# A streaming-encoder block on one core: the first weights behind two token tiles, the first products in three passes, and half of one remainder on GpSimd

## The chip, the cores and the metric

The kernel runs on one core of a Trainium2 chip. The time is that of one launch in device microseconds, the median of several runs. The engines run side by side, each through a list of its own, and meet only at semaphores: TensorE (PE in the profile, its weight loads PEld), VectorE (DVE), ScalarE (ACT), GpSimd (POOL) and SyncE (SP), which issues the DMAs.

## The reference

512 tokens of 1024 features pass one layer. All tensors are float32.

```
u = RMSNorm(h)                                    # 512 x 1024
q, k, v, z, xBC, dt, gate_a, gate_b = split(u @ w_in)
A = banded attention with sinks(rope(q), rope(k), v) @ w_attn_out
B = (SSD scan over silu(conv(xBC)), dt; y * silu(z), group RMSNorm) @ w_ssd_out
h = h + RMSNorm(merge(A, B) @ w_out)
f = silu(conv(gate)) * conv(value), of RMSNorm(h) @ w_up
h = h + RMSNorm(f @ w_down)
```

## The kernel before

**Products in three parts.** Each float32 operand is split into a rounded part and the remainder. Of the weights these are `whi` (rounded by ScalarE, a copy of `raw`, L452) and `wlo` (VectorE subtracts, `raw` minus `whi`, L797), of the normed tokens `uhi` and `ulo`. Every product is three matmuls: rounded by rounded, remainder by rounded, rounded by remainder (L1204 to L1206 where the tokens are the stationary operand, L1197 to L1199 where the weights are).

**Weight blocks.** The weights come in blocks of at most 128x2048, numbered through the whole kernel, into two slots in turn. Per block: SyncE loads it, ScalarE rounds it (`hi`), VectorE takes the remainder (`lo`), TensorE multiplies. Semaphores count them: `hi_done`, `lo_done`, `blk_done`. SyncE waits for `lo_done` before it loads into a slot again, ScalarE for `blk_done` before it overwrites one.

**The groups.** The mixer runs in four groups (`G`), each of seven blocks: 0 and 1 are q, k, v (in group 0 also dt), 2 to 4 the convolved columns, 5 and 6 the gate z, where block 5 holds the first half of the contraction and block 6 the second. After block 4 a group goes through four token tiles of 128 (`t`). In tile 0 TensorE does, in this order: transposes `tok(0)` and `tok(1)`, sums of decays, the products of z with block 5, the attention scores, transposes `tok(2)` to `tok(4)` (L1319), the products of z with block 6, and the products `y` (L1416), which need `decay_m` after its mask (L968) and `xdt` (L974). `tok(4)` needs `silu(5)` and the masked `cb_m` from VectorE.

**The work beside it in tile 0.** VectorE finishes the convolutions (`taps`, L899), multiplies `silu` (L908: `tanh_c` by `conv`), builds `cb_m` (L959), masks `decay_m` twice, takes the remainder of block 6 (`lo_next(5)`), and then does softmax and `xdt`. ScalarE: `tanh`, `tok` copies, exponentials, the rounding of block 6 (`hi_next(5)`). GpSimd: the products `seg_lo` (`build`, L386), two for each tile, then `xdtd` and `xd` (L406, L408).

**The beginning.** SyncE issues two tiles of x, small parameters, two more tiles of x, and then block 0 (four DMAs). Per token tile: ScalarE squares, GpSimd takes the inverse root (`root_x`), VectorE scales (`scale_x`, L823), TensorE transposes (L1214), VectorE applies the norm's weight (`weigh_x`, L812), ScalarE rounds (`u_hi`, L463), and VectorE (first four feature blocks, `rest_x`, L819) and GpSimd (last four, L374) take the remainder. GpSimd also works out the angles for rope (L358 to L369) on which ScalarE's sines wait (L488, semaphore `ang_ok`). After these ScalarE does `hi_next(1)`, the rounding of block 2.

Of the kernel before, what the change touches and what calls it, by code (L numbers as in the profile page):

```python
# [21 lines left out]
def hybrid_block(nc, x, positions, mix_pre_norm, w_in, attn_sinks, ssd_conv_w, ssd_conv_b, ssd_dt_bias,  # L22
# [47 lines left out]
    with ctx:  # L70
# [86 lines left out]
        for name in (  # L157
            "x_in0", "x_in1", "x_in2", "x_in3", "consts_in", "par_in", "par2_in", "posT_ok", "pool_c", "loaded0", "loaded1", "hi_done", "lo_done", "blk_done",
            "band_zero", "dve_chain", "pool_chain", "xsq", "rstd", "xn", "xT_mm", "u_plain", "uhi_ok", "u_ok", "u2_ok", "parT_mm", "par_ok",
            "ang_ok", "rope_tab", "hp_ok",  # L160
            "qkv_mm", "qkv_sb", "roped", "va_ok", "dtabs", "dtexp", "dt_ok", "decay_mm", "decay_ok",
            "qkT_mm", "qkT_sb", "conv_mm", "tapped", "conv_ok", "tanhed", "silu_ok", "tok_mm", "tok_sb",
            "seg_hi_ok", "seg_lo_ok", "seg_mm", "lexp", "cb_mm", "cbm_ok", "s_mm", "smx", "sexp", "p_ok", "z_mm", "ztanh", "zg_ok",
            "m_ok", "pT_mm", "pT_sb", "y_mm", "y_done", "xdt_ok", "xdtd_ok", "xd_ok", "st_mm", "st_ok", "w_ok", "wsq",
            "yrstd", "yn_ok", "yT_mm", "yT_sb", "o_mm", "o_sb",
            "split_hi", "split_lo", "ga_mm", "ga_tanh", "at_mm", "at_ok", "gb_mm", "gb_tanh", "so_mm", "so_ok",
            "mg_hi", "mg_lo", "mg_lo2", "res_in", "out_mm", "d_sq", "d_rstd", "d_h", "h_sq", "h_rstd", "hn_ok", "hT_mm", "h_plain", "h_hi", "h_ok",
            "up_mm", "ftap", "fconv", "ftanh", "f_ok", "fhi_ok", "flo_ok", "fpar_ok", "dn_mm", "e_sq", "e_rstd", "e_ok", "stored",
        ):
# [139 lines left out]
        def _(pool):  # L309
# [44 lines left out]
            w0, w1 = tanh_c[:, 0, :], tanh_c[:, 1, :]
            NA = NT * HALF
            r3 = lambda a: a.rearrange("p (t k) -> p t k", t=NT)
            pool.wait_ge(s["posT_ok"], 1)
            link(pool.tensor_tensor(r3(w0[:, 0:NA]), small[:, 12:16].unsqueeze(2).to_broadcast([P, NT, HALF]),  # L358
                                    inv[:, :].unsqueeze(1).to_broadcast([P, NT, HALF]), ALU.mult))
            link(pool.tensor_scalar(w1[:, 0:NA], w0[:, 0:NA], 1.0 / 6.283185307179586, MAGIC, ALU.mult, ALU.add))  # L360
            link(pool.tensor_scalar(w1[:, 0:NA], w1[:, 0:NA], -MAGIC, None, ALU.add))
            for c in TWO_PI:
                link(pool.tensor_scalar(w1[:, NA:2 * NA], w1[:, 0:NA], -c, None, ALU.mult))
                link(pool.tensor_tensor(w0[:, 0:NA], w0[:, 0:NA], w1[:, NA:2 * NA], ALU.add))
            link(pool.tensor_scalar(w0[:, 0:NA], w0[:, 0:NA], PI, -PI, ALU.min, ALU.max))
            link(pool.tensor_scalar(w1[:, 0:NA], w0[:, 0:NA], 0.0, None, ALU.min))
            link(pool.tensor_scalar(w1[:, NA:2 * NA], w0[:, 0:NA], 0.0, None, ALU.max))
            link(pool.tensor_tensor(w1[:, NA:2 * NA], w1[:, NA:2 * NA], w1[:, 0:NA], ALU.subtract))
            pool.tensor_scalar(w0[:, NA:2 * NA], w1[:, NA:2 * NA], -1.0, 1.5707963267948966, ALU.mult, ALU.add).then_inc(s["ang_ok"], 1)  # L369

            for t in range(NT):
                pool.wait_ge(s["uhi_ok"], t + 1)
                c = slice(t * P, (t + 1) * P)
                pool.tensor_tensor(ulo[:, KD // 2:, c], plain(t)[:, KD // 2:, :], uhi[:, KD // 2:, c].bitcast(F32),  # L374
                                   ALU.subtract).then_inc(s["u2_ok"], 1)
# [408 lines left out]
        def _(dve):  # L784
# [101 lines left out]
            def group(i, p):  # L886
# [300 lines left out]
        def _(pe):  # L1187
# [41 lines left out]

            pe.wait_ge(s["par2_in"], 16 * 10)  # L1230
            pe.wait_ge(s["u_plain"], 2)
            pe.transpose(ps[:, 3, 0:NR1], prow[0:NR1, 1, :], ident[0:NR1, 0:NR1]).then_inc(s["parT_mm"], 1)
            pe.transpose(ps[:, 3, NR1:NR1 + P], prow[:, 2, :], ident[:, :]).then_inc(s["parT_mm"], 1)
            pe.transpose(ps[:, 3, NR1 + P:NR1 + P + NCP], prow[0:NCP, 0, :], ident[0:NCP, 0:NCP]).then_inc(s["parT_mm"], 1)

# [6 lines left out]
            def group(i, p):  # L1242
# [381 lines left out]
```

## Time and profile before

| | |
|---|---|
| median of 3 runs | 1083.49 us (1082.47 to 1083.94) |
| the profiled execution: its own time | 1083.09 us |
| its span, first to last instruction | 1081.4 us |
| TensorE busy | 1051.6 us, 97% |
| VectorE, ScalarE, GpSimd busy | 649.9, 454.6, 130.7 us |
| mean granted TensorE clock | 0.996 |

Read it so: the profiled execution lies 0.4 us under the median of the runs, and its span 1.7 us under its own time. TensorE is idle for under 30 us in all, so what another engine does counts only where TensorE waits for it.

### The profile page before, as it was taken

Reading aid. Unit: us, or ns where it says so; the run is one execution under the profiler, and the core shown is the slowest. Engines: PE = TensorE matmul, PEld = TensorE weight load, DVE = VectorE, ACT = ScalarE, POOL = GpSimd, SP = SyncE. Lnnn points to the kernel's source line nnn. Section 1 sums busy time; section 2 is a strip of 40 time slices with the busy share of each in tenths; the row PEclk is TensorE's granted clock in tenths of the full one; section 3 lists DMA queues with packets and bytes.
Section 4 is the critical chain, followed back from the end, with each engine's and each line's share of the span. In section 5 each row is a group of like instructions: output and inputs, shape, how many; then the busy total and the mean of one; then the engine's idle time right before and its main releaser. Section 6 shows DMA issues by size and latency. Waiting matters only on the chain.

```text
span 1081.4 us, 13741 instructions
## 1 busy us (share of the span) xinstructions
PE 1051.6 (97%) x5295; PEld 883.5 (82%) x5295; DVE 649.9 (60%) x863; ACT 454.6 (42%) x714; POOL 130.7 (12%) x200
## 2 busy tenths in 40 slices
PE   6999999999999999999999999999999999999997
PEld 5987887888779877888888888788888888888886
DVE  6788777876776777842433233466666666651214
ACT  6465456536654565532321213363434444431112
POOL 7113300330043013200000003120000000000001
PEclk8999999999999999999999999999999999999999
DMA  6321132114202420233233343412423333333221
GB/s 190 116 68 30 40 118 68 30 40 122 82 12 62 134 78 2 78 98 97 78 117 97 97 162 130 136 40 78 113 81 110 84 107 87 104 96 111 82 75 78
DMA packets 108426, 95.39 MB, mean 88 GB/s; under 512 B 12175, under 2 KB 98523, under 8 KB 108379
## 3 DMA queue, kind: packets, MB, share of 16 engines
q1 hardware_dynamic: 108379, 94.74, 28.8%
q8 instruction: 32, 0.52, 0.2%
q14 instruction: 15, 0.12, 0.0%
HBM read 92.63 MB, written 2.10 MB: 88 GB/s over the span
## 4 chain that ended last, share of the span: by engine, by line
PE 91%; DVE 5%; ACT 2%; DMA 1%; issue 1%; POOL 0%; DVEq 0%; POOLq 0%; SPq 0%; ACTq 0%
PE ps L1197 18%; PE ps L1199 18%; PE ps L1198 18%; PE ps L1204 9%; PE ps L1206 9%; PE ps L1205 9%; PE ps L1416 3%; DVE wlo L797 1%; PE ps L1412 1%; PE ps L1364 1%; PE ps L1428 1%; PE ps L1437 1%; DVE conv L899 1%; DVE conv L908 1%; PE ps L1239 1%
## 5 line engine op out<-in xcount | busy, mean ns | idle before, releaser
L797 DVE TENSOR_TENSOR wlo<-raw,whi 128x2048 fp32r<-128x2048 f32 (+2 forms) x83 | 188.7, 2275 | 213.2 <-ACT whi L452 213.2
L1197 PE MATMUL ps<-uhi,whi 128*128 128x512 f32 x640 | 249.6, 390 | 0.0
L1199 PE MATMUL ps<-uhi,wlo 128*128 128x512 f32 x640 | 249.1, 389 | 0.0
L1198 PE MATMUL ps<-ulo,whi 128*128 128x512 f32 x640 | 249.0, 389 | 0.0
L452 ACT ACTIVATE whi<-raw 128x2048 fp32r<-128x2048 f32 (+2 forms) x83 | 155.2, 1871 | 173.4 <-PE ps L1206 93.0
L1199 PEld LDWEIGHTS ps<-uhi,wlo 128*128 128x128 f32 x640 | 120.1, 188 | 25.0
L1197 PEld LDWEIGHTS ps<-uhi,whi 128*128 128x128 f32 x640 | 120.1, 188 | 24.8 <-DVE wlo L797 0.2
L1198 PEld LDWEIGHTS ps<-ulo,whi 128*128 128x128 f32 x640 | 120.1, 188 | 24.7
L1204 PE MATMUL ps<-whi,uhi 128*128 128x512 f32 (+2 forms) x320 | 122.2, 382 | 9.9 <-DVE wlo L797 9.9
L1206 PE MATMUL ps<-wlo,uhi 128*128 128x512 f32 (+2 forms) x320 | 119.3, 373 | 0.0
L1205 PE MATMUL ps<-whi,ulo 128*128 128x512 f32 (+2 forms) x320 | 119.2, 373 | 0.0
L1145 DVE SCALAR_TENSOR_TENSOR yT<-ps,fpar,yT 128x511 f32<-128x511 f32 x88 | 65.7, 749 | 37.6 <-ACT yT L754 36.0
L1204 PEld LDWEIGHTS ps<-whi,uhi 128*128 128x128 f32 x320 | 60.9, 190 | 18.2 <-ACT x_tok L521 8.8
L754 ACT ACTIVATE yT<-ps,fpar 128x512 f32<-128x512 f32 x44 | 34.2, 780 | 98.9 <-DVE fpar L1140 68.0
L1197 PE MATMUL ps<-rhi,whi 128*128 128x512 f32 x192 | 74.8, 390 | 0.0
L1199 PE MATMUL ps<-rhi,wlo 128*128 128x512 f32 x192 | 74.7, 389 | 0.0
L1198 PE MATMUL ps<-rlo,whi 128*128 128x512 f32 x192 | 74.7, 389 | 0.0
L1204 PE MATMUL ps<-whi,rhi 128*128 128x512 f32 x176 | 68.5, 389 | 0.0
L1205 PE MATMUL ps<-whi,rlo 128*128 128x512 f32 x176 | 68.5, 389 | 0.0
L1206 PE MATMUL ps<-wlo,rhi 128*128 128x512 f32 x176 | 68.5, 389 | 0.0
L1206 PEld LDWEIGHTS ps<-wlo,uhi 128*128 128x128 f32 x320 | 60.9, 190 | 7.9
L1205 PEld LDWEIGHTS ps<-whi,ulo 128*128 128x128 f32 x320 | 61.0, 191 | 7.0
(220 smaller groups left out, 1437.7 us busy)
## 6 DMA issues: line engine op xcount, KB each, us to landing
raw<-in_w_in_dram SPq DMA_DIRECT2D x24, 1024.0 KB
raw<-in_w_up_dram SPq DMA_DIRECT2D x44, 512.0 KB
raw<-in_w_down_dram SPq DMA_DIRECT2D x11, 1024.0 KB
raw<-in_w_in_dram SPq DMA_DIRECT2D x16, 512.0 KB
raw<-in_w_ssd_out_dram SPq DMA_DIRECT2D x8, 1024.0 KB
raw<-in_w_attn_out_dram SPq DMA_DIRECT2D x4, 1024.0 KB
raw<-in_w_out_dram SPq DMA_DIRECT2D x4, 1024.0 KB
yT<-in_x_dram SPq DMA_DIRECT2D x4, 512.0 KB, 5.2
```

What stands on the lines that cost most here:

```text
L452: act.activation(whi[sl][:, 0:width] if into is None else into, raw[sl][:, 0:width], ACT.Copy).then_inc(s["hi_done"], 1)
L754: act.activation(work[:, v, :], bank(2 * q + v), ACT.Identity, scale=fpar[:, q, FTAPS - 1, v:v + 1], bias=fpar[:, q, FTAPS, v:v + 1]).then ...
L797: dve.tensor_tensor(wlo[sl][:, 0:width] if into is None else into, raw[sl][:, 0:width], h.bitcast(F32), ALU.subtract).then_inc(s["lo_done" ...
L899: ins = dve.scalar_tensor_tensor(out=conv[:, f, sh:], in0=ps[:, 4 + f % 4, 0:S - sh], scalar=cw[:, k, at:at + 1], in1=conv[:, f, sh:], op0 ...
L1145: ins = dve.scalar_tensor_tensor(out=work[:, v, sh:], in0=ps[:, 2 * q + v, 0:S - sh], scalar=fpar[:, q, k, v:v + 1], in1=work[:, v, sh:], ...
L1197: pe.matmul(bank(b)[:, span], hi_[:, k, c], ah[:, span], start=first and k == 0, stop=False)
L1198: pe.matmul(bank(b)[:, span], hi_[:, k, c], al[:, span], start=False, stop=False)
L1199: ins = pe.matmul(bank(b)[:, span], lo_[:, k, c], ah[:, span], start=False, stop=last and k == KD - 1)
L1204: pe.matmul(o, ah, wh, start=first, stop=False)
L1205: pe.matmul(o, al, wh, start=False, stop=False)
L1206: return pe.matmul(o, ah, wl, start=False, stop=last)
L1416: ins = pe.matmul(ps[:, 5 if t else 6, c_], decay_m[:, h, :], xdt[:, c_], start=True, stop=True)
```

## The change

**In the groups.** ScalarE rounds block 6 right after `tok(0)` (`hi_next(5)`), ahead of `tanh(5)`, `tok(1)` and the exponentials. VectorE takes the remainder of the first half of that block alone (1024 of 2048 columns), between `silu(4)` and `silu(5)`; GpSimd takes that of the other half, between `build(0)` and `build(1)`, and counts in `zlo2_ok`. TensorE waits for `zlo2_ok` before the products with block 6, and SyncE before it loads into that slot.

**At the beginning.** Block 0 is issued ahead of token tiles 2 and 3. Its remainder is split between VectorE and GpSimd (832 columns each). TensorE's products with block 0 go tile by tile in three passes of four matmuls, with the transposes of tiles 2 and 3 and of the parameters between them. ScalarE rounds block 0 ahead of its squares of tiles 2 and 3. GpSimd works `root_x`, its part of the token remainders (L356 after the change), the half block and the angles in a new order, with the large memset first.

```diff
@@ SyncE, put(n)
+                if n == 2:
+                    sp.wait_ge(s["wlo0_ok"], 1)
+                if n <= N_C1 + 1 and n % PER_G == 1 and n > 1:
+                    sp.wait_ge(s["zlo2_ok"], n // PER_G)
@@ SyncE, beginning
-            for t in range(2, NT):
-                sp.dma_start(xin[:, t, :], x2[t * P:(t + 1) * P, :]).then_inc(x_in[t], 16)
...
                     if g == 0 and h == 0:
+                        for t in range(2, NT):
+                            sp.dma_start(xin[:, t, :], x2[t * P:(t + 1) * P, :]).then_inc(x_in[t], 16)
                         late_parameters()
@@ GpSimd, beginning
+            root_x(0)
+            root_x(1)
+            pool.wait_ge(s["posT_ok"], 1)
...
+            pool.wait_ge(s["hi_done"], 1)
+            half = slice(2 * QKV0, 4 * QKV0)
+            pool.tensor_tensor(wlo[0][:, half], raw[0][:, half], whi[0][:, half].bitcast(F32), ALU.subtract).then_inc(s["wlo0_ok"], 1)
+            root_x(2)
+            rest_x(0)
+            root_x(3)
+            rest_x(1)
+            for n, c in enumerate(TWO_PI):
+                link(pool.tensor_scalar(w1[:, NA:2 * NA], w1[:, 0:NA], -c, None, ALU.mult))
+                link(pool.tensor_tensor(w0[:, 0:NA], w0[:, 0:NA], w1[:, NA:2 * NA], ALU.add))
+                if n:
+                    rest_x(n + 1)
@@ GpSimd, group
                 build(0)
+                sl = (G * PER_G + 6) % 2
+                pool.wait_ge(s["hi_done"], G * PER_G + 7)
+                pool.tensor_tensor(wlo[sl][:, BLK // 2:], raw[sl][:, BLK // 2:], whi[sl][:, BLK // 2:].bitcast(F32),
+                                   ALU.subtract).then_inc(s["zlo2_ok"], 1)
@@ ScalarE, beginning
+            hi(0, 64, None, 4 * QKV0)
             square_x(2)
+            u_hi(0)
             square_x(3)
-            u_hi(0)
-            hi(0, 64, None, 4 * QKV0)
             u_hi(1)
+            u_hi(2)
@@ ScalarE, group
                 tok(0)
+                hi_next(5)
+                tanh(5)
                 act.wait_ge(s["xd_ok"], G * NT)
                 tok(1)
-                tanh(5)
...
                     if t == 0:
-                        hi_next(5)
@@ VectorE, beginning
             weigh_x(0)
+            weigh_x(1)
             scale_x(2)
+            rest_x(0)
+            lo(0, 1, 2 * QKV0)
             scale_x(3)
-            weigh_x(1)
-            rest_x(0)
-            lo(0, 1, 4 * QKV0)
+            rest_x(1)
             weigh_x(2)
-            rest_x(1)
             weigh_x(3)
@@ VectorE, group
                 silu(4)
+                lo_next(5, BLK // 2)
                 silu(5)
...
                         mask_decays(range(2))
-                        lo_next(5)
@@ TensorE, beginning, first_block()
+                pe.wait_ge(s["hi_done"], 1)
+                rounded_rounded(0)
+                rest_rounded(0)
+                rounded_rounded(1)
+                turn_x(2)
+                pe.wait_ge(s["lo_done"], 1)
+                pe.wait_ge(s["wlo0_ok"], 1)
+                rounded_rest(0)
+                rest_rounded(1)
+                rounded_rest(1)
+                turn_x(3)
+                turn_parameters()
+                rounded_rounded(2)
+                rest_rounded(2)
+                rounded_rest(2)
...
+                rounded_rounded(3)
+                rest_rounded(3)
+                rounded_rest(3).then_inc(s["blk_done"], 1)
@@ TensorE, group
                             sl = block_ready(5 + h)
+                            if h:
+                                pe.wait_ge(s["zlo2_ok"], G + 1)
```

How VectorE's list stands in group 0 around tile 0, before (L797 is the remainder of block 6, L908 silu, L959 `cb_m`, L968 the masks, L985 the start of softmax):

```order
L899 SCALAR_TENSOR_TENSOR conv<-ps,par,conv 128x509
L908 SCALAR_TENSOR_TENSOR conv<-tanh_c,conv 128x512 x2
L959 TENSOR_TENSOR cb_m<-ps,tri 128x128
L968 TENSOR_TENSOR decay_m<-decay_m,cb_m 128x512 x2
L797 TENSOR_TENSOR wlo<-raw,whi 128x2048
L985 MEMSET ps 64x2x2x64
L986 TENSOR_REDUCE sm<-ps 128x4
```

and the same place after the change:

```order
L915 SCALAR_TENSOR_TENSOR conv<-ps,par,conv 128x509
L924 SCALAR_TENSOR_TENSOR conv<-tanh_c,conv 128x512
L813 TENSOR_TENSOR wlo<-raw,whi 128x1024
L924 SCALAR_TENSOR_TENSOR conv<-tanh_c,conv 128x512
L976 TENSOR_TENSOR cb_m<-ps,tri 128x128
L985 TENSOR_TENSOR decay_m<-decay_m,cb_m 128x512 x2
L1001 MEMSET ps 64x2x2x64
```

The remainder has moved from behind the masks to between the two `silu`, at half its width.

GpSimd's list in group 0, from the first two tiles' `seg_lo` on, before:

```order
L386 TENSOR_TENSOR seg_lo<-tri,adt_lo 128x512 x4
L406 TENSOR_TENSOR xdtd<-xdt,dec 128x512
L408 TENSOR_TENSOR xd<-x_tok,hp 128x512
L412 TENSOR_SCALAR small<-small 128x1
L416 TENSOR_TENSOR small<-small 128x1
```

and after:

```order
L399 TENSOR_TENSOR seg_lo<-tri,adt_lo 128x512 x2
L408 TENSOR_TENSOR wlo<-raw,whi 128x1024
L399 TENSOR_TENSOR seg_lo<-tri,adt_lo 128x512 x2
L423 TENSOR_TENSOR xdtd<-xdt,dec 128x512
L425 TENSOR_TENSOR xd<-x_tok,hp 128x512
```

The other half of the remainder stands between the two `seg_lo` of tile 0 and the two of tile 1, which now come after it.

TensorE's list at the beginning, after the transposes of the small parameters; before it is 32 transposes of x (L1214), three of the parameters, then 48 matmuls in threes. After the change (L1230 are the transposes of x, L1256 rounded by rounded, L1261 remainder by rounded, L1265 rounded by remainder):

```order
L1230 MATMUL ps<-ident,yT 128x128 x16
L1256 MATMUL ps<-whi,uhi 128x416 x4
L1261 MATMUL ps<-whi,ulo 128x416 x4
L1256 MATMUL ps<-whi,uhi 128x416 x4
L1230 MATMUL ps<-ident,yT 128x128 x8
L1265 MATMUL ps<-wlo,uhi 128x416 x4
L1261 MATMUL ps<-whi,ulo 128x416 x4
L1265 MATMUL ps<-wlo,uhi 128x416 x4
L1230 MATMUL ps<-ident,yT 128x128 x8
L1292 MATMUL ps<-ident,prow 128x72
```

Products with tiles 0 and 1 now stand ahead of the transposes of tiles 2 and 3.

## Rows read from the trace of the kernel before

**Rows 1.** The page: busy time of each engine over the span

```profile
PE 1051.6 (97%) x5295; PEld 883.5 (82%) x5295; DVE 649.9 (60%) x863; ACT 454.6 (42%) x714; POOL 130.7 (12%) x200
```

**Rows 2.** What TensorE waited for, whole span: us in total, times, longest

```profile
PE ps L1204 <- DVE wlo L797: 9.9, 5, 2.0
```

**Rows 3.** Timeline, group 0, tile 0: start us, us, engine, line, idle before

```profile
75.83 0.60 ACT L521 ACTIVATE x_tok<-ps 128x512 f32<-128x512 f32 x1
...
76.01 2.04 POOL L386 TENSOR_TENSOR seg_lo<-tri,adt_lo 128x512 fp32r<-128x512 f32 x2 [16.62 <-PE ps L1342]
...
78.80 1.92 ACT L452 ACTIVATE whi<-raw 128x2048 fp32r<-128x2048 f32 x1
...
79.73 1.47 PE L1319 MATMUL ps<-ident,conv 128*128 128x128 f32 x12
...
80.75 2.29 DVE L797 TENSOR_TENSOR wlo<-raw,whi 128x2048 fp32r<-128x2048 f32 x1
...
83.19 0.47 PE L1204 MATMUL ps<-whi,uhi 128*128 128x512 f32 x1 [1.99 <-DVE wlo L797]
...
85.13 0.69 DVE L974 TENSOR_TENSOR xdt<-x_tok,dt_s 128x512 f32<-128x512 f32 x1
...
86.04 1.90 PE L1416 MATMUL ps<-xdt,decay_m 128*128 128x64 f32 x16
```

**Rows 4.** Timeline at three places where VectorE and GpSimd overlap

```profile
77.01 1.04 POOL L386 TENSOR_TENSOR seg_lo<-tri,adt_lo 128x512 fp32r<-128x512 f32 x1
...
77.20 1.40 DVE L908 SCALAR_TENSOR_TENSOR conv<-tanh_c,conv 128x512 f32<-128x512 f32 x1
...
86.85 0.73 DVE L1001 TENSOR_TENSOR probs<-probs,sm 128x512 f32<-128x512 f32 x1
...
86.99 1.49 POOL L408 TENSOR_TENSOR xd<-x_tok,hp 128x512 f32<-128x512 f32 x1
...
441.61 2.28 DVE L797 TENSOR_TENSOR wlo<-raw,whi 128x2048 fp32r<-128x2048 f32 x1
...
441.83 2.96 POOL L406 TENSOR_TENSOR xdtd<-xdt,dec 128x512 f32<-128x512 f32 x1 [5.39 <-DVE xdt L974]
```

**Rows 5.** Timeline near 15 us: two VectorE operations in a row, one of GpSimd waiting

```profile
15.23 0.67 DVE L819 TENSOR_TENSOR ulo<-yT,uhi 128x512 fp32r<-128x512 f32 x1
...
15.42 0.89 POOL L361 TENSOR_SCALAR tanh_c<-tanh_c 128x128 f32<-128x128 f32 x1
...
15.83 1.97 DVE L797 TENSOR_TENSOR wlo<-raw,whi 128x1664 fp32r<-128x1664 f32 x1
```

**Rows 6.** Durations: groups by form (busy us, mean ns), and L797 by itself (min/median/max)

```profile
L374 POOL TENSOR_TENSOR ulo<-yT,uhi 128x512 fp32r<-128x512 f32 x4 | 5.0, 1288 | 0.0
L364 POOL TENSOR_TENSOR tanh_c<-tanh_c 128x128 f32<-128x128 f32 x3 | 1.5, 487 | 0.3
L968 DVE TENSOR_TENSOR decay_m<-decay_m,cb_m 128x512 f32<-128x512 f32 x32 | 21.5, 684 | 0.4
L797 DVE TENSOR_TENSOR wlo<-raw,whi x83: 1750/2291/2590, 15.8 to 1055.9; 128x2048 fp32r<-128x2048 f32 x75, 128x1536 fp32r<-128x1536 f32 x6, 128x1664 fp32r<-128x1664 f32 x2
```

**Rows 7.** Timeline of the beginning

```profile
5.96 1.06 ACT L457 ACTIVATE yT<-yT 128x1024 f32<-128x1024 f32 x1 [0.27 <-DMA yT<-in_x_dram]
...
9.36 1.06 ACT L457 ACTIVATE yT<-yT 128x1024 f32<-128x1024 f32 x1 [0.16 <-DMA yT<-in_x_dram]
...
11.91 1.59 ACT L452 ACTIVATE whi<-raw 128x1664 fp32r<-128x1664 f32 x1
...
17.90 0.69 PE L1204 MATMUL ps<-whi,uhi 128*128 128x416 f32 x1 [1.98 <-DVE wlo L797]
...
25.63 0.31 ACT L488 ACTIVATE sinT<-tanh_c 128x128 f32<-128x128 f32 x1 [1.81 <-POOL tanh_c L369]
```

**Rows 8.** Windows of 1 us: busy us of PE, PEld, DVE, ACT, POOL, then granted clock, DMA share, GB/s

```profile
23.00:24.00 1.00, 1.00 (x5) 0.97 (x4) 1.00 (x2) 0.81 (x1) 0.83 (x3) 0.60 0.47 119
```

**Rows 9.** Timeline from the end of block 0 to the start of block 2

```profile
31.12 1.91 ACT L452 ACTIVATE whi<-raw 128x2048 fp32r<-128x2048 f32 x1
...
33.13 2.29 DVE L797 TENSOR_TENSOR wlo<-raw,whi 128x2048 fp32r<-128x2048 f32 x1 [2.50 <-ACT whi L452]
...
39.23 0.39 PE L1197 MATMUL ps<-uhi,whi 128*128 128x512 f32 x1
```

More of the change, by code:

```diff
@@ L342, in root_x, with rest_x @@
                 inverse_root(small[:, 8 + t:9 + t], small[:, 4 + t:5 + t], 1.0 / D, "rstd")
-            for t in range(NT):
-                root_x(t)
             pool.memset(qB[:, :, :], 0.0).then_inc(s["band_zero"], 1)
+            w0, w1 = tanh_c[:, 0, :], tanh_c[:, 1, :]
+            NA = NT * HALF
+            r3 = lambda a: a.rearrange("p (t k) -> p t k", t=NT)
+            def rest_x(t):
+                pool.wait_ge(s["uhi_ok"], t + 1)
+                c = slice(t * P, (t + 1) * P)
+                pool.tensor_tensor(ulo[:, KD // 2:, c], plain(t)[:, KD // 2:, :], uhi[:, KD // 2:, c].bitcast(F32),
+                                   ALU.subtract).then_inc(s["u2_ok"], 1)
+            root_x(0)
+            root_x(1)
+            pool.wait_ge(s["posT_ok"], 1)
+            link(pool.tensor_tensor(r3(w0[:, 0:NA]), small[:, 12:16].unsqueeze(2).to_broadcast([P, NT, HALF]),
+                                    inv[:, :].unsqueeze(1).to_broadcast([P, NT, HALF]), ALU.mult))
+            link(pool.tensor_scalar(w1[:, 0:NA], w0[:, 0:NA], 1.0 / 6.283185307179586, MAGIC, ALU.mult, ALU.add))
+            link(pool.tensor_scalar(w1[:, 0:NA], w1[:, 0:NA], -MAGIC, None, ALU.add))
+            pool.wait_ge(s["hi_done"], 1)
[10 more added lines that the diff above has]
+                    rest_x(n + 1)
+            link(pool.tensor_scalar(w0[:, 0:NA], w0[:, 0:NA], PI, -PI, ALU.min, ALU.max))
+            link(pool.tensor_scalar(w1[:, 0:NA], w0[:, 0:NA], 0.0, None, ALU.min))
+            link(pool.tensor_scalar(w1[:, NA:2 * NA], w0[:, 0:NA], 0.0, None, ALU.max))
+            link(pool.tensor_tensor(w1[:, NA:2 * NA], w1[:, NA:2 * NA], w1[:, 0:NA], ALU.subtract))
+            pool.tensor_scalar(w0[:, NA:2 * NA], w1[:, NA:2 * NA], -1.0, 1.5707963267948966, ALU.mult, ALU.add).then_inc(s["ang_ok"], 1)
             pool.wait_ge(s["band_zero"], 1)
@@ L352, in _ @@
             pool.wait_ge(s["band_zero"], 3)
[L354 to L375, printed above, removed]
             base = count[0]
@@ L482, in _ @@
             act.activation(fcw[:, :, :].rearrange("p k t -> p (k t)")[:, 0:P], ps[:, 3, NR1:NR1 + P], ACT.Copy).then_inc(s["par_ok"], 1)
-            u_hi(2)
+            u_hi(3)
             hi(1, 64, None, 4 * QKV0)
-            u_hi(3)
             act.wait_ge(s["ang_ok"], 1)
@@ L1222, in _, with turn_x @@
             pe.transpose(ps[:, 7, KD:KD + NT], rtmp[0:NT, 0:P], ident[0:NT, 0:NT]).then_inc(s["parT_mm"], 1)
-            for t in range(NT):
+            def turn_x(t):
                 pe.wait_ge(s["xn"], t + 1)
@@ L1228, in _, with first_block, tile, rounded_rounded @@
                 turn_tile(t, xin[:, t, :], "xT_mm")
[L1230 to L1234, printed above, removed]
+            def first_block():
+                wh, wl = (w[0][:, 0:4 * QKV0].rearrange("p (k n) -> p k n", k=4) for w in (whi, wlo))
+                def tile(t):
+                    return slice(t * P, (t + 1) * P)
+                def rounded_rounded(t):
+                    pe.wait_ge(s["uhi_ok"], t + 1)
+                    for k in range(4):
+                        pe.matmul(bank(t, QKV0), uhi[:, k, tile(t)], wh[:, k, :], start=k == 0, stop=False)
+                def rest_rounded(t):
+                    pe.wait_ge(s["u_ok"], t + 1)
+                    for k in range(4):
+                        pe.matmul(bank(t, QKV0), ulo[:, k, tile(t)], wh[:, k, :], start=False, stop=False)
+                def rounded_rest(t):
+                    for k in range(4):
+                        ins = pe.matmul(bank(t, QKV0), uhi[:, k, tile(t)], wl[:, k, :], start=False, stop=False)
+                    return ins
+                pe.wait_ge(s["hi_done"], 1)
[13 more added lines that the diff above has]
+                rounded_rest(2)
+                pe.wait_ge(s["par_ok"], 5)
+                rounded_rounded(3)
+                rest_rounded(3)
+                rounded_rest(3).then_inc(s["blk_done"], 1)
@@ L1236, in turn_y @@
+            turn_x(1)
             def turn_y(b):
@@ L1252, in group @@
                 for h in range(2):
+                    if G == 0 and h == 0:
+                        first_block()
+                        turn_y(7)
+                        continue
                     sl = block_ready(h)
@@ L1259, in group @@
                             pe.wait_ge(s["zg_ok"], G * NT)
-                        if h == 0 and t == NT - 1:
-                            pe.wait_ge(s["par_ok"], 5)
                         for k in range(4):
```

9 lines of the change are left out of this document (8 added, 1 removed).

## The prediction

> **What bounds the kernel now.** I read the page first: TensorE is busy 1051.6 of 1081.4 us [rows 1], so time comes or goes only where TensorE waits. Then the list of what it waited for: 9.9 us in five waits for the remainder of a weight block [rows 2]. One of them, 1.98 us, is at the beginning [rows 7]; the other four, 7.9 us together, are one per group, the 1.99 us ahead of the products with block 6 [rows 3]. Last the timelines of these two places. In tile 0 the chain is: ScalarE rounds block 6 from 78.80 to 80.72, VectorE takes the remainder from 80.75 to 83.04, TensorE has been idle since 81.20 (when `tok(4)` ended) and goes on at 83.19. Behind it stands a second chain: VectorE's softmax and `xdt`, which end 2.78 us after the remainder (85.13 + 0.69 = 85.82), and `y` starts at 86.04 [rows 3]. So products with block 6 and VectorE's chain end nearly together: if block 6 came earlier by itself, `y` would still wait for VectorE.
>
> **The groups, without interference.** ScalarE can round block 6 from about 75.85 (where `tok(1)` starts now [rows 3]) to 77.77. The half remainder costs VectorE less: from 1750 ns for 1536 columns and 2291 for 2048 [rows 6] a column costs 1.06 ns, so 1024 cost 2.29 - 1.08 = 1.21 us. GpSimd's other half: 1288 ns for 512 columns and 487 for 128 [rows 6] give 2.09 ns a column, so 1.29 + 1.07 = 2.36 us. If they ran freely, both halves would be there by 80.2, TensorE would lose no time before block 6, and `y` would start at about 84.15: 1.9 us earlier, 7.6 us in four groups.
>
> **The groups, with interference.** They do not run freely. `silu(4)` on VectorE, which takes 0.68 alone, took 1.40 us because it started at 77.20 while a `seg_lo` of GpSimd ran from 77.01 to 78.05; it ended 0.55 after that one. Conversely `xdtd` of GpSimd took 2.96 instead of 1.04 when VectorE's subtraction had started before it, and ended 0.90 after that had ended at 443.89 [rows 4]. So the two shut each other out for a whole instruction, and a hand-over saves 0.13 of the second. The masks never overlap GpSimd in this trace; nearest is a multiply of the same form, with a broadcast second input: it started at 86.85, and `xd` of GpSimd, begun at 86.99, took 1.49 for 1.04 [rows 4]. I take it that masks are shut out too. The Trainium skill (SBUF — State Buffer, Who interferes with whom) says the same of any VectorE instruction with two SBUF inputs against a GpSimd one that reads SBUF, and that whichever issues first holds the ports to its end; by it the masks contend and `cb_m`, which reads PSUM, does not. If the masks did not, the sum below would be smaller by two `seg_lo`, about 2 us in a group.
>
> Who goes first when both wait? GpSimd's L361 began at 15.42 during one VectorE operation, and the next, L797, began at 15.83. It was L361 that got through, at 16.31, long before L797 ended at 17.80; L797 took 1.97 where 1.06 ns a column make 1.88 [rows 5, 6]. So they take turns. The turns after the change, beginning with the end of `silu(4)` at 77.88 (77.20 + 0.68, now unhindered since `build(1)` is behind the half block): VectorE's half 1.21, to 79.09; GpSimd's half 2.36, to 81.45; `silu(5)` 0.68, to 82.13; `seg_lo` 1.04, to 83.17; mask 0.68, to 83.85; `seg_lo` 1.04, to 84.89; mask 0.68, to 85.57; the chain to the end of `xdt`, 2.78, to 88.35. Six hand-overs at 0.13 give back 0.8: 87.55. `y` then starts at 87.65, 1.6 us later than at 86.04 now. If GpSimd's half goes first instead, the same pieces stand in another order and the sum stays. TensorE waits twice in it: `tok(4)`, which needs `silu(5)` and `cb_m`, near 82.2 instead of 80.7, and then `y`, for `xdt`, since the products with block 6 (2.8 us) are done by 85.5. Behind `y` the attention probabilities are late by as much as `xdt` and are wanted no sooner, so the 1.6 us stay: four groups, **6.4 us slower**. Moving `seg_lo` is part of it: before, it lay at 76.01 to 78.05 [rows 3], mostly beside taps that read PSUM; now it costs two turns among the masks.
>
> The first rounding costs nothing more on ScalarE: `tanh(5)` ends near 78.4 and `tok(1)` near 79.0, ahead of `tok(2)` at 79.73 [rows 3]. SyncE's new waits cost nothing: the block behind is used only after a whole tile loop. The added semaphore wait on TensorE is for an event that the turns above already carry.
>
> **The beginning.** Block 0 no longer stands behind tiles 2 and 3 of x. These took from 5.96 to 9.36 on ScalarE's view of their landing, 3.4 us; block 0 was rounded from 11.91, when it had landed [rows 7]. So it lands near 8.5, and is rounded by 10.1; tile 2 of x then lands near 10.3. From there: square (1.25), `u_hi(0)` to 12.65, first pass from 12.7 instead of 17.90. But the next steps are chained: GpSimd's half block to 12.1, `root_x(2)` to 13.0, its own remainder of tile 0 (1.29) ahead of VectorE's scaling of tile 2, which shares the ports, to 14.9; VectorE's `rest_x(0)` to 15.6, so the second pass starts near 15.6; transposes of tile 2 near 18.5; and `weigh_x`, `u_hi`, `rest_x` of tiles 2 and 3, 1.2 + 1.1 + 0.7 each and one behind the other, let the last passes start near 25.5 and end near 29.3. The clock bears on this too: TensorE's granted clock rose inside 23 to 24 us [rows 8], until then a matmul of 416 columns takes twice as long. I let it rise near 20.4. Block 1 would start near 29.8, about 0.5 us earlier than before.
>
> What is late next is the rounding of block 2. It starts at 31.12 behind the sines, which started at 25.63 [rows 7, 9]. The angles are now spread between GpSimd's remainders, the last of which waits for `u_hi(3)` near 25.9; five operations follow, shut out by VectorE's subtraction of block 1. I put the sines at 31.9, 6.3 later, the rounding at about 34.7, the remainder at 36.6 to 38.9. TensorE needs it at 39.23 [rows 9], or 38.8 with the earlier start. The cover is nearly used up; without it each further us costs one. So the beginning gives **0.3 us**. Its bounds: nothing hidden and a late clock, 1.5 us lost; every wait short and the clock early, 2 us won (more the block 2 chain forbids).
>
> **Sum.** 1083.09 + 6.4 - 0.3 = 1089.2 for an execution like the profiled one; the median of the runs is 0.4 above that one, so 1089.6 us.
>
> **The rivals.** Turns (forecast), 55%: 1089.6, with 1.5 us for the beginning and 0.4 a group for the hand-overs its own range is 1086.5 to 1093.
> VectorE keeps the ports while it has work that needs them, 15%: its half and `silu(5)` run through to 79.7, GpSimd's half then to 81.9, block 6 starts 1.2 us early, but the masks come after it and `xdt` ends near 85.9, as now. Groups at 0.0, total 1083.2 to 1083.5. Against it speaks L361 [rows 5].
> Free running, 15%: the interference is small or falls into gaps, and the wait for block 6 is simply gone: 1083.5 - 7.6 - 0.3 = 1075.6. It holds if GpSimd's half block is over by about 80.2 and neither mask is held up. For it speaks only that most GpSimd work now costs nobody time; against it [rows 4].
> The clock falls in the longer waits of tile 0, 10%: idle 1.5 and then some 2.1 us with 3 us of work between. TensorE's waits of 1.99 us now [rows 3] never did it, but each fall would cost a few us (at the beginning TensorE ran at half clock up to 23.6 [rows 8]): with one or two falls 1092 to 1097.
> The beginning alone going wrong, 5%: block 2 late by 2 us or more, 1092.
>
> **How the numbers follow.** A measurement of this kernel tells about 0.2%, 2.2 us, from no change. Faster is free running and a little of the second case with a good beginning: 0.17. Same is the rest of the second and the edge of the first: 0.15. Slower: 0.68. The range 1079 to 1094.5 leaves out most of free running below and the worst clock case above, under 2 in 10 together.
>
> **What would show it.** In the profile after: VectorE's `silu(5)` at over 1.5 us, or GpSimd's half block at well over 2.4; `seg_lo` of tile 1 and the masks alternating; TensorE's wait for `wlo` in the groups gone, and in its place waits at `tok(4)` and at `y`, over 3 us a group. I am wrong in the main step if the masks keep 0.68 beside `seg_lo`, or if `silu(5)` starts before GpSimd's half block.

## The result

The changed kernel takes 1095.93 us (median of 4 runs, 1095.13 to 1096.85) against 1083.03 us before: 12.9 us slower, ratio 1.0119 (95% interval 1.0101 to 1.0136). The direction was forecast; the size (1089.6, range 1079 to 1094.5) was not.

The page of the changed kernel, span and busy times, against [rows 1]:

```profile
span 1093.4 us, 13762 instructions
PE 1057.2 (97%) x5295; PEld 886.1 (81%) x5295; DVE 653.6 (60%) x863; ACT 454.6 (42%) x714; POOL 149.6 (14%) x205
```

The span grew by 12.0 us. TensorE has as many matmuls as before, yet is busy 5.6 us longer: part of its work ran slower. What TensorE waited for, against [rows 2]:

```profile
PE ps L1483 <- DVE xdt L991: 8.3, 4, 2.1
PE ps L1384 <- DVE cb_m L976: 5.4, 4, 1.4
PE ps L1261 <- DVE ulo L835: 2.4, 2, 1.5
PE ps L1256 <- ACT uhi L480: 1.7, 1, 1.7
```

The waits for a weight remainder are gone. In their place each group has two, at `tok(4)` (L1384) and at `y` (L1483): 13.7 us in all where there were 7.9. The timeline of tile 0 in group 0, against [rows 3] (L813 is VectorE's half, L408 GpSimd's, L924 `silu`, L399 `seg_lo`, L985 the masks, L991 `xdt`):

```profile
78.16 0.68 DVE L924 SCALAR_TENSOR_TENSOR conv<-tanh_c,conv 128x512 f32<-128x512 f32 x1
...
78.76 1.22 DVE L813 TENSOR_TENSOR wlo<-raw,whi 128x1024 fp32r<-128x1024 f32 x1
78.78 3.40 POOL L408 TENSOR_TENSOR wlo<-raw,whi 128x1024 fp32r<-128x1024 f32 x1 [17.85 <-ACT whi L469]
...
79.90 2.84 DVE L924 SCALAR_TENSOR_TENSOR conv<-tanh_c,conv 128x512 f32<-128x512 f32 x1
...
82.16 2.93 POOL L399 TENSOR_TENSOR seg_lo<-tri,adt_lo 128x512 fp32r<-128x512 f32 x2
...
82.66 0.28 DVE L976 TENSOR_TENSOR cb_m<-ps,tri 128x128 f32<-128x128 f32 x1
83.04 2.59 DVE L985 TENSOR_TENSOR decay_m<-decay_m,cb_m 128x512 f32<-128x512 f32 x2
...
87.71 0.69 DVE L991 TENSOR_TENSOR xdt<-x_tok,dt_s 128x512 f32<-128x512 f32 x1
```

Read it by ends: VectorE's half ends at 79.98, GpSimd's at 82.18, `silu(5)` at 82.74. The first `silu` took 0.68; the second stands as 2.84 and ended 0.56 after GpSimd's half, so most of its 2.84 is waiting. `cb_m`, which reads PSUM, takes 0.28 beside a running `seg_lo`. TensorE in the same stretch:

```profile
88.55 1.97 PE L1483 MATMUL ps<-xdt,decay_m 128*128 128x64 f32 x16 [2.08 <-DVE xdt L991]
90.33 0.56 PE L1406 MATMUL ps<-seg_hi,above 128*128 128x512 f32 x1
90.68 0.63 PE L1407 MATMUL ps<-seg_lo,above 128*128 128x512 f32 x1
91.10 0.63 PE L1406 MATMUL ps<-seg_hi,above 128*128 128x512 f32 x1
```

The matmuls of 512 columns start 0.43 us apart instead of the usual 0.23. Windows of the changed kernel (busy PE, PEld, DVE, ACT, POOL, then the granted clock) show why:

```profile
86.00:89.00 3.00, 0.92 (x7) 0.53 (x6) 2.80 (x6) 1.81 (x5) 0.43 (x1) 1.00 0.15 33
89.00:92.00 3.00, 3.00 (x19) 2.54 (x19) 2.50 (x6) 0.00 (x0) 2.07 (x2) 0.76 0.02 5
92.00:95.00 3.00, 3.00 (x23) 1.75 (x21) 1.11 (x2) 0.60 (x1) 0.00 (x0) 0.67 0.00 0
...
200.50:202.50 2.00, 2.00 (x7) 1.18 (x5) 0.96 (x2) 0.60 (x1) 0.00 (x0) 0.50 0.00 0
...
308.00:312.00 4.00, 3.85 (x33) 2.65 (x32) 2.92 (x5) 1.28 (x3) 0.89 (x1) 1.00 0.02 4
...
415.50:418.00 2.50, 2.50 (x10) 2.01 (x10) 1.71 (x3) 0.00 (x0) 0.63 (x1) 0.50 0.02 7
```

TensorE's clock is at 2.4 GHz through the wait ahead of `y` and falls to 1.2 GHz at 90.6, just behind the sixteen small matmuls of `y`, in groups 0, 1 and 3, not in 2. The two windows of group 0 give its length: 2 x 3 x (0.24 + 0.33) = 3.4 us at half speed, so 1.7 us lost. At the beginning TensorE starts block 2 at 40.19, against 39.23 in [rows 9].

The account: waits in the groups 13.7 - 7.9 = 5.8, beginning 1.0, three falls of the clock 3 x 1.7 = 5.1. Sum 11.9 of the 12.0 us. The starts of `y` in groups 1, 2 and 3 (88.55 in group 0), and of `y` in group 1 before (86.04 in group 0), check it without counting waits:

```profile
197.47 1.97 PE L1483 MATMUL ps<-xdt,decay_m 128*128 128x64 f32 x16 [2.08 <-DVE xdt L991]
...
306.37 1.97 PE L1483 MATMUL ps<-xdt,decay_m 128*128 128x64 f32 x16 [2.09 <-DVE xdt L991]
...
413.62 2.53 PE L1483 MATMUL ps<-xdt,decay_m 128*128 128x64 f32 x16 [2.08 <-DVE xdt L991]
```

```profile
191.68 1.91 PE L1416 MATMUL ps<-xdt,decay_m 128*128 128x64 f32 x16
```

From one `y` to the next it was 105.64 us before. Now it is 107.25 behind group 2, where the clock stays up, and 108.92 and 108.90 behind groups 0 and 1, where it falls. So the turns cost 1.6 us a group, and a fall costs 1.7. Counted this way the parts add up to about half a microsecond more than the 12.0.

### The profile page after: what moved, and what is told of

Read it like the earlier page. It is cut to its first block, busy times and chain, and to the rows that moved or that the text cites. A ratio compares the mean times of both kernels' runs of the same rounds, so it can differ in the third digit from the quotient of the medians.

```text
span 1093.4 us, 13762 instructions
## 1 busy us (share of the span) xinstructions
PE 1057.2 (97%) x5295; PEld 886.1 (81%) x5295; DVE 653.6 (60%) x863; ACT 454.6 (42%) x714; POOL 149.6 (14%) x205
## 4 chain that ended last, share of the span: by engine, by line
PE 89%; DVE 6%; ACT 2%; DMA 1%; issue 1%; POOL 1%; SPq 0%; DVEq 0%; POOLq 0%; ACTq 0%
PE ps L1213 18%; PE ps L1215 18%; PE ps L1214 18%; PE ps L1220 8%; PE ps L1222 8%; PE ps L1221 8%; PE ps L1483 3%; DVE conv L924 1%; PE ps L1495 1%; PE ps L1479 1%; PE ps L1429 1%; PE ps L1504 1%; DVE decay_m L985 1%; DVE conv L915 1%; PE ps L1406 1%
## 5 line engine op out<-in xcount | busy, mean ns | idle before, releaser
L813 DVE TENSOR_TENSOR wlo<-raw,whi 128x2048 fp32r<-128x2048 f32 (+3 forms) x83 | 183.5, 2212 | 210.0 <-ACT whi L469 209.9
L1214 PE MATMUL ps<-ulo,whi 128*128 128x512 f32 x640 | 249.0, 389 | 0.0
L1214 PEld LDWEIGHTS ps<-ulo,whi 128*128 128x128 f32 x640 | 120.2, 188 | 24.6
L1220 PE MATMUL ps<-whi,uhi 128*128 128x512 f32 (+2 forms) x304 | 115.2, 379 | 0.0
L1222 PE MATMUL ps<-wlo,uhi 128*128 128x512 f32 (+2 forms) x304 | 112.7, 371 | 0.0
L1221 PE MATMUL ps<-whi,ulo 128*128 128x512 f32 (+2 forms) x304 | 112.6, 370 | 0.0
L1214 PE MATMUL ps<-rlo,whi 128*128 128x512 f32 x192 | 74.7, 389 | 0.0
L915 DVE SCALAR_TENSOR_TENSOR conv<-ps,par,conv 128x511 f32<-128x511 f32 (+2 forms) x72 | 53.8, 748 | 20.9 <-ACT conv L520 19.2
L1222 PEld LDWEIGHTS ps<-wlo,uhi 128*128 128x128 f32 x304 | 57.1, 188 | 7.8
L1220 PEld LDWEIGHTS ps<-whi,uhi 128*128 128x128 f32 x304 | 57.1, 188 | 7.1
```

What stands on the lines that cost most here:

```text
L813: dve.tensor_tensor(wlo[sl][:, 0:width] if into is None else into, raw[sl][:, 0:width], h.bitcast(F32), ALU.subtract).then_inc(s["lo_done" ...
L915: ins = dve.scalar_tensor_tensor(out=conv[:, f, sh:], in0=ps[:, 4 + f % 4, 0:S - sh], scalar=cw[:, k, at:at + 1], in1=conv[:, f, sh:], op0 ...
L1214: pe.matmul(bank(b)[:, span], hi_[:, k, c], al[:, span], start=False, stop=False)
L1220: pe.matmul(o, ah, wh, start=first, stop=False)
L1221: pe.matmul(o, al, wh, start=False, stop=False)
L1222: return pe.matmul(o, ah, wl, start=False, stop=last)
```

## The experiments

Ratios are to runs of the kernel before on the same chip. "The group change alone" (e2) is the base of several.

**e1: the new beginning alone.** All edits in the groups undone.

> The new beginning alone; the four groups stand as before. My theory of the result splits the 12 us of the changed kernel into about 1.0 us from the beginning (block 2 started at 40.19 instead of 39.23), 4 x 1.6 us of turns in tile 0, and about 3 x 1.7 us of half clock behind the new waits. By it this kernel is 1.0 us slower than before (0.5 to 1.5), block 2 starts near 40.2, the four 1.99 us waits for block 6 are back, and the clock does not fall in any group. Rival: the beginning is what costs, through something carried into the groups: then 5 us or more slower. My recorded forecast for it was 0.3 us faster.

Measured: 1083.91 us, ratio 1.0006 (0.9995 to 1.0018); block 2 starts at 39.90, the four waits are back (7.9 us), the clock does not fall in a group. That is under the 1.0 us expected. So the beginning costs little or nothing; it is not where the 12.9 us are. Whether it is 0.5 us better or 1.9 worse this run does not tell.

**e2: the group change alone.** The kernel before, with the edits of `hi_next(5)`, `lo_next(5, BLK // 2)`, GpSimd's half block and its waits.

> The group change alone; the beginning stands as before. Theory: 4 x 1.5 to 1.6 us of turns, plus 1.7 us for each fall of the clock, of which there may be 0 to 4 in an execution (3 in the profiled one of the changed kernel): 6 to 13 us slower, likeliest 11. TensorE waits 1.35 at tok(4) and 2.08 at y in each group. Rival (free running, and the loss came from the beginning): 7 us faster.

Measured: 1095.32 us, ratio 1.0108 (1.0091 to 1.0124). TensorE waits 5.4 us in four for `cb_m` and 8.3 in four for `xdt`, as in the changed kernel, and the clock falls for 3.4 us behind `y` in groups 1, 2 and 3. The groups alone carry the loss. "Free running" is out.

**e3: VectorE takes the whole remainder at the new place.**

```diff
-                lo_next(5, BLK // 2)
+                lo_next(5)
```
and GpSimd's half and the waits for it removed.

> As the group change alone, but VectorE takes the whole remainder of block 6 between silu(4) and silu(5), and GpSimd none of it (the beginning as before). Theory (the loss comes from GpSimd's half and the seg_lo behind it shutting VectorE out): VectorE's chain from silu(4) to xdt is then the same work in another order, seg_lo of tile 1 lies beside the taps again, y starts within 0.3 us of before, total within 2 us of before, unless the clock falls in the waits. Rival (it is the early rounding on ScalarE, or the remainder ahead of silu(5), that costs): as slow as the group change alone, 6 us or more.

Measured: 1082.42 us, ratio 0.9987 (0.9975 to 1.0000). The same early rounding and the same place ahead of `silu(5)` cost nothing once GpSimd is out of it:

```profile
78.20 2.28 DVE L797 TENSOR_TENSOR wlo<-raw,whi 128x2048 fp32r<-128x2048 f32 x1
...
80.41 0.68 DVE L908 SCALAR_TENSOR_TENSOR conv<-tanh_c,conv 128x512 f32<-128x512 f32 x1
...
81.39 1.29 DVE L969 TENSOR_TENSOR decay_m<-decay_m,cb_m 128x512 f32<-128x512 f32 x2
```

The whole remainder on VectorE ends at 80.48, 2.28 us after it began; in the changed kernel the last part of it, GpSimd's half, ended 3.42 after VectorE's half began (82.18 - 78.76). Handing half of it over made the block ready later. TensorE waits 1.0 us at `tok(4)` and 0.8 at `y` here, 7.0 in four groups where it was 7.9, and the clock falls in no group.

**e4: more work for TensorE.** The changed kernel, with eight matmuls into a bank nobody reads, ahead of `y` in tile 0:

```diff
+                    if t == 0:
+                        pe.wait_ge(s["lexp"], T * 2 + 2)
+                        for k in range(8):
+                            pe.matmul(bank(2), uhi[:, k, c], tiles(whi[block_ready(6)][:, :], 4)[:, k % 4, :], start=True, stop=True)
                     pe.wait_ge(s["m_ok"], T * 2 + 2)
```

> The changed kernel with 8 more matmuls of 512 columns per group (32 in all) behind the products with block 6 of tile 0, into a bank that nobody reads, so that TensorE works through 1.8 us of the 2.08 us wait ahead of y. More work, same dependencies. Theory (the clock falls because the wait and the sparse stretch of small matmuls behind it come together): no granted clock of 0.5 in the groups, y starts where it did, and the kernel is about 5 us faster than the changed one, so about 7 us slower than before. Rival (the clock events are chance, or set by something else): still falls, no faster than the changed kernel, 12 us slower than before.

Measured: 1089.31 us, ratio 1.0052 (1.0035 to 1.0068): 32 matmuls more than the changed kernel and, by the medians, 6.6 us faster. `y` starts where it did, and nothing behind it is slow:

```profile
86.45 1.98 PE L1478 MATMUL ps<-whi,uhi 128*128 128x512 f32 x8
88.68 1.97 PE L1487 MATMUL ps<-xdt,decay_m 128*128 128x64 f32 x16 [0.25 <-DVE xdt L991]
90.46 0.47 PE L1406 MATMUL ps<-seg_hi,above 128*128 128x512 f32 x1
90.77 0.39 PE L1407 MATMUL ps<-seg_lo,above 128*128 128x512 f32 x1
91.00 0.40 PE L1406 MATMUL ps<-seg_hi,above 128*128 128x512 f32 x1
```

The clock falls in no group, and from one `y` to the next it is 107.25 to 107.27 us, as in the changed kernel where the clock stays up. The clock's part is shown. What is left, 5.7 us by the medians, is what the forecast had for turns and beginning together: 6.1.

**e5: GpSimd's half left out.** e2 without GpSimd's subtraction and the waits for it; the second half of that buffer is stale, so 1024 columns of one remainder per group are not computed.

> The group change alone, with GpSimd's half of the remainder of block 6 left out: TensorE multiplies with whatever the other half of that buffer held, so 1024 columns of one remainder per group are not computed. The waits for it go too. seg_lo of tile 1 lies beside the taps again. It shows what the change would have brought if GpSimd's half had cost VectorE nothing. Theory (turns): silu(5) 0.68 us, no wait at tok(4), y starts 1.5 to 1.9 us earlier than in the kernel before, 6 to 7.5 us faster in all. Rival (the early rounding or the place of the half is what costs): slower than before by 3 us or more.

Measured: 1078.18 us, ratio 0.9959 (0.9945 to 0.9973): 5 us faster, under the 6 to 7.5 expected. No wait at `tok(4)`, 0.8 us left at `y`. This is what the change would have brought had the half cost VectorE nothing, less than the 7.6 us I had worked out, as VectorE's chain still bounds `y`.

**e6: the half as memsets.** GpSimd writes the same 1024 columns twice and reads nothing; that half of the remainder is zero.

```diff
-                pool.tensor_tensor(wlo[sl][:, BLK // 2:], raw[sl][:, BLK // 2:], whi[sl][:, BLK // 2:].bitcast(F32),
-                                   ALU.subtract).then_inc(s["zlo2_ok"], 1)
+                pool.memset(wlo[sl][:, BLK // 2:].bitcast(F32), 0.0).then_inc(s["band_zero"], 1)
+                pool.wait_ge(s["band_zero"], 4 + G)
+                pool.memset(wlo[sl][:, BLK // 2:].bitcast(F32), 0.0).then_inc(s["zlo2_ok"], 1)
```

> The group change alone, with GpSimd's subtraction replaced by two memsets of the same 1024 columns, 0.9 us each, so that it is held for nearly as long but reads nothing from SBUF; the half of the remainder is zero instead of computed. Everything else, the order and the waits, is as in the group change. Theory (it is the reading that shuts VectorE out, not GpSimd being late): VectorE's half 1.1 to 1.2, silu(5) 0.68 beside the memsets, only the seg_lo behind them still take turns with the masks; y about 1.5 us earlier than in the group change alone, total 0 to 3 us slower than before. Rival (GpSimd's time or any GpSimd work blocks): silu(5) over 2 us again, 9 us or more slower.

Measured: 1087.56 us, ratio 1.0037 (1.0022 to 1.0051): 4.3 us slower than before, where 0 to 3 was expected. The clock fell here too, in groups 2 and 3, behind waits of 1.7 us ahead of `y` and with none at `tok(4)`.

```profile
77.69 1.22 DVE L804 TENSOR_TENSOR wlo<-raw,whi 128x1024 fp32r<-128x1024 f32 x1
77.69 0.96 POOL L397 MEMSET wlo<- 128x1024 f32 x1 [18.41 <-ACT whi L459]
...
78.71 0.95 POOL L399 MEMSET wlo<- 128x1024 f32 x1
78.82 0.68 DVE L915 SCALAR_TENSOR_TENSOR conv<-tanh_c,conv 128x512 f32<-128x512 f32 x1
...
79.62 2.49 POOL L388 TENSOR_TENSOR seg_lo<-tri,adt_lo 128x512 fp32r<-128x512 f32 x2
79.81 2.85 DVE L976 TENSOR_TENSOR decay_m<-decay_m,cb_m 128x512 f32<-128x512 f32 x2
```

Both engines start at 77.69 and neither delays the other; `silu(5)` takes 0.68 beside the second memset. For these VectorE operations, which have two inputs in SBUF, it is GpSimd's reading that holds them up, not its being busy. Behind it the masks still take 2.85 with `seg_lo`: the second contention by itself.

**e7: `seg_lo` of tile 1 after the masks.** e2, with GpSimd waiting for both masks ahead of `build(1)`. Everything is computed.

```diff
                         pool.wait_ge(s["seg_mm"], T * 2 + 2)
+                        if t == 0:
+                            pool.wait_ge(s["m_ok"], T * 2 + 2)
                         build(t + 1)
```

> The group change alone, with seg_lo of tile 1 on GpSimd held back until both masks are done. Everything is computed. Theory: each mask is 0.68 again, y starts 1.7 to 2.0 us earlier than in the group change alone, so about where it did before; the wait ahead of y shrinks from 2.08 to under 0.6 and the clock does not fall there: within 2 us of before. Rival (seg_lo in turns costs nothing, it is GpSimd's half alone): y where it was, 10 us slower than before.

Measured: 1084.08 us, ratio 1.0010 (1.0000 to 1.0019): one wait more, and 11 us of e2's 12 are back.

```profile
77.65 3.41 POOL L397 TENSOR_TENSOR wlo<-raw,whi 128x1024 fp32r<-128x1024 f32 x1 [18.43 <-ACT whi L460]
...
78.77 2.85 DVE L916 SCALAR_TENSOR_TENSOR conv<-tanh_c,conv 128x512 f32<-128x512 f32 x1
...
81.92 1.29 DVE L977 TENSOR_TENSOR decay_m<-decay_m,cb_m 128x512 f32<-128x512 f32 x2
```

`silu(5)` still pays for the half block, the masks are free again (1.29 for two), TensorE's wait ahead of `y` goes from 2.1 to 0.8 us, and the clock falls in no group. The `seg_lo` in turns cost 1.3 us a group directly; the rest, about as much again, goes with the clock that no longer falls.

**e11: the wait in another place.** The kernel before; only the order of the twelve matmuls with block 6 in tile 0 is changed, so that the eight which need `whi` alone come first.

> The kernel before, with only this: in tile 0 the products with block 6 start with the 8 matmuls that need only its rounded part, then the 4 that need the remainder. Nothing on VectorE, ScalarE or GpSimd moves. y still waits for xdt, so the wait of about 2 us that TensorE has per group only changes its place, from ahead of the products with block 6 (dense work behind it) to ahead of y (small matmuls behind it). Theory of the clock: the place matters, the clock now falls for 3.4 us behind the wait in one to four groups, 1.7 us each: y where it was, 2 to 7 us slower than before though no work was added. Rival (only the length of a wait or chance matters): no falls in the groups, same as before within 1 us.

Measured: 1087.56 us, ratio 1.0039 (1.0019 to 1.0059), single runs from 1082.67 to 1092.22. TensorE's wait is shorter than the 1.99 us before:

```profile
81.92 1.20 PE L1407 MATMUL ps<-wlo,uhi 128*128 128x512 f32 x4
84.78 2.43 PE L1425 MATMUL ps<-xdt,decay_m 128*128 128x64 f32 x16 [1.67 <-DVE xdt L974]
86.97 0.77 PE L1341 MATMUL ps<-seg_hi,above 128*128 128x512 f32 x1
87.55 0.63 PE L1342 MATMUL ps<-seg_lo,above 128*128 128x512 f32 x1
```

but it now has the small matmuls behind it instead of twelve dense ones, and the granted clock reads so in groups 0, 2 and 3:

```profile
86.50:89.00 2.50, 2.50 (x9) 2.01 (x9) 1.87 (x3) 0.00 (x0) 0.80 (x1) 0.50 0.00 0
...
299.00:302.00 3.00, 3.00 (x14) 2.81 (x14) 1.58 (x4) 0.00 (x0) 1.15 (x1) 0.50 0.02 6
408.00:411.00 3.00, 3.00 (x13) 2.71 (x13) 1.90 (x4) 0.00 (x0) 1.02 (x1) 0.50 0.01 2
```

A wait of 1.67 us ahead of the small matmuls loses the clock, one of 1.99 us ahead of dense work did not. From one `y` to the next:

```profile
192.03 1.97 PE L1425 MATMUL ps<-xdt,decay_m 128*128 128x64 f32 x16 [1.67 <-DVE xdt L974]
...
297.64 3.56 PE L1425 MATMUL ps<-xdt,decay_m 128*128 128x64 f32 x16 [1.66 <-DVE xdt L974]
```

Behind group 1, where the clock stays up, it is 105.61 us, as before the edit; behind group 0 107.25. In groups 2 and 3 the clock stays down for 6.8 us, and behind group 2 it is 108.86. So the edit by itself costs nothing, and what it loses goes with the falls. That the runs spread by 9.5 us because falls differ in number and length is likely, but only one execution has a trace.

All traces together show how far the place explains it. Behind waits of 1.66 us or more ahead of `y` (changed kernel, e2, e6, e11) the clock fell in 11 of 16 groups; behind the waits of 1.99 us ahead of the products with block 6 (before, e1) in 0 of 8; behind waits of 0.8 us or less ahead of `y` (e3, e4, e5, e7) in 0 of 16. Something else has a part in it. In a stretch that no edit touched stands one more wait, near 700 to 715 us (L1214 in the kernel before, 2.0 us up to 703.8). The clock fell within 1 us of its end in e2, e6, e10 and e11, with waits of 2.0 to 2.3 us, and not in the eight other traces, with 1.0 to 2.4. Why one execution falls there and another does not stays open.

**e9: `xdt` of tile 0 on GpSimd, with the order of e11.**

```diff
+                    if t == 0:
+                        pool.wait_ge(s["tok_sb"], G * 5 + 5)
+                        pool.tensor_tensor(view(xdt), x_tok[:, t, :].rearrange("p (h d) -> p h d", h=SH), bc(dt_s[:, t, group_heads(G)]),
+                                           ALU.mult).then_inc(s["xdt_ok"], 1)
```

> A version meant to beat both, built on the kernel before: in tile 0 the products with block 6 run in passes, those that need only its rounded part first (8 matmuls, 1.85 us), so they start when ScalarE is done; and xdt of tile 0 is GpSimd's, at a place where VectorE reads PSUM. Expected: the 1.99 us wait at block 6 gone, y starts near 84.2 instead of 86.04, TensorE then waits 0.7 us for the attention probabilities, 1.1 to 1.4 us won in each group, 4 to 5.5 us in all. Rival (turns between xdt on GpSimd and VectorE's subtraction and small operations eat it): within 1.5 us of before.

Measured: 1081.87 us, ratio 0.9992 (0.9982 to 1.0002): 1.4 us by the medians, not clear of no change, where 4 to 5.5 was expected. The rival had it: a VectorE operation on 4 columns, 0.16 us by itself, was shut out by `xdtd`.

```profile
82.64 1.04 POOL L410 TENSOR_TENSOR xdtd<-xdt,dec 128x512 f32<-128x512 f32 x1
82.73 0.97 DVE L991 TENSOR_TENSOR sm<-sm,sinks 128x4 f32<-128x4 f32 x1
```

**e10: e9 with `xdtd` of tile 0 held back.**

```diff
+                        pool.wait_ge(s["smx"], T + 1)
                     pool.wait_ge(s["xdt_ok"], T + 1)
```

> The version with xdt of tile 0 on GpSimd, with one more wait: GpSimd begins xdtd of tile 0 only when VectorE is through with the front of its softmax, so the small VectorE operation that took 0.97 us behind xdtd takes 0.16 again. Expected: the attention probabilities are ready 0.6 to 0.8 us earlier per group, TensorE's wait for them goes from 1.4 to 0.7 us, 2.5 to 3 us faster than without it, so about 4 us faster than before. Rival (the chain is bound elsewhere): as without it, 1 us faster than before.

Measured: 1080.30 us, ratio 0.9976 (0.9967 to 0.9985). The small operation takes 0.16 again, and TensorE waits 3.6 us in four for the probabilities instead of 5.7. Less than the 4 us expected, but this computes everything and beats both kernels: 2.3 us under the one before and, by the ratios, about 15 under the changed one.

```profile
83.42 0.16 DVE L992 TENSOR_TENSOR sm<-sm,sinks 128x4 f32<-128x4 f32 x1
```

## Why the prediction was right in its mechanism and wrong in its size

- **Turns on the ports: right.** Forecast: `y` 1.6 us late per group, 6.4 in all. Measured: 88.55 - 86.04 = 2.51 in group 0, of which 0.96 came from the beginning: 1.55; 1.6 from one `y` to the next where the clock stays up; the waits grew by 5.8 us in all. From the end of `silu(4)` to the end of `xdt` the forecast had 9.67 us, the trace 9.56 (78.84 to 88.40). The pieces hold too: GpSimd's half ended 2.20 after VectorE's (2.36 less a hand-over of 0.13), then `silu(5)`, `seg_lo`, mask, `seg_lo`, mask. e3, e5, e6 and e7 each took one link out, and in each the waits that it had caused shrank or went. That GpSimd, waiting, goes ahead of a VectorE operation that comes later was read from one place [rows 5]; `silu(5)` confirmed it in all four groups, at 2.84 to 2.85 us, with each half block at 3.40 to 3.41.
- **The masks contend: right.** Taken from a multiply of like form [rows 4]; 2.59 for two here, 2.85 in e6.
- **TensorE's two waits: right.** `tok(4)` and `y` were named as the places, "over 3 us a group"; they are 1.35 and 2.08.
- **The clock: the step that failed.** I put falls in the longer waits among the rivals, at 10%, with this reason: "TensorE's waits of 1.99 us now [rows 3] never did it". That compared lengths, and the sum had nothing for the clock in the groups. What the runs showed is that the place matters: the old wait had twelve matmuls of 512 columns behind it, the new one the sixteen of 64 columns of `y`. The fall came in 3 of 4 groups of the profiled run, 5.1 us of the 5.9 between the forecast 1089.2 and the 1095.1 of that execution. e4 takes it away, e11 makes it without anything else.
- **The beginning: a term of small size with the wrong sign.** Forecast 0.3 us won; in the profile block 2 starts 0.96 us late, in e1 0.67, and by time e1 can't be told from before. In the kernel before, the clock rose at 23.8 by the 0.60 of [rows 8], not at 23.6. The landing (rounded from 9.12, forecast 8.5) and the chain were about right. The clock again was not: I let it rise near 20.4; four matmuls of 416 columns took 1.74 us at 20.69 and 0.91 at 23.03, so it rose near 22.3, about 1 us lost against the forecast. (The clock view of that trace and of e4's begins only there and counts what lies ahead as full speed, so mean clocks of different executions don't compare.) The chain of the angles was late as forecast (sines at 33.30, forecast 31.9; rounding of block 2 at 35.74, remainder to 40.03, forecast 38.9), and the cover just held.
- **The range** left out the clock's full effect because I priced one or two falls, at a tenth. The measured 1095.9 lies in that rival's 1092 to 1097; it came by three falls in the profiled run, at 1.7 us each.

## What to carry to other kernels

Work moved from VectorE to GpSimd is only off VectorE's path while the two don't shut each other out. In these traces they ran side by side where VectorE read an input from PSUM (the taps, `cb_m`), and where GpSimd only wrote beside a VectorE operation with two inputs in SBUF. That VectorE reads only one input from SBUF is not enough by itself. In the kernel before, VectorE's scaling of a token tile, 0.74 us alone, took 2.26 beside GpSimd's large memset and ended after it:

```profile
10.74 0.74 DVE L823 TENSOR_SCALAR yT<-yT,small 128x1024 f32<-128x1024 f32 x1
...
11.84 1.80 POOL L347 MEMSET qB<- 128x2048 f32 x1
...
11.92 2.26 DVE L823 TENSOR_SCALAR yT<-yT,small 128x1024 f32<-128x1024 f32 x1 [0.44 <-POOL small L337]
```

So look the pair up in a trace, list both engines' operations for the stretch and add them up in turns before moving anything, four-column operations and what stands behind the moved one on GpSimd included. When a wait of TensorE changes its place, look at what stands behind it: a wait ahead of dense matmuls costs its length, the same wait ahead of small ones can cost the clock as well, and a few idle matmuls in it can be cheaper than none. Where TensorE waits, ask first which of its matmuls need the late operand at all; moving them alone only moves the wait (e11).

## What was not expected of the hardware

- A wait of 1.67 us followed by small matmuls brought TensorE's granted clock from 2.4 to 1.2 GHz (e11), and 32 matmuls more made a kernel 6.6 us faster (e4). The falls did not come in every group, and in e6 and e11 some lasted 6.8 us instead of 3.4.
- GpSimd's memset of 128x1024 and VectorE's subtraction with two inputs in SBUF started together and took 0.96 and 1.22 us (e6), the subtraction as in e5, where it took 1.21 with no GpSimd work beside it. With a GpSimd operation that reads, either waits for the other's end. The memset did hold up VectorE's scaling with one input (2.26 us for 0.74).
- The time that the profile gives an operation includes its turn: 2.84 us for `silu(5)` and 0.97 for one on 4 columns are waits, not work.
